# Stick-breaking attention in a long one-core kernel: mask added to the logits, inclusive sums, twelve blocks in three banks, numbered steps, output product by chunks

## What is computed

```python
z = jnp.einsum('bqkgd,bskd->bkgqs', qb, kf)          # qb is scaled by 1/8
mask = key_pos[None, :] < q_pos[:, None]
log_1m_beta = jnp.where(mask, jax.nn.log_sigmoid(-z), 0.0)
rev = lax.cumsum(log_1m_beta, axis=4, reverse=True)
excl = jnp.concatenate([rev[..., 1:], jnp.zeros_like(rev[..., :1])], axis=-1)
a = jnp.where(mask, jnp.exp(jax.nn.log_sigmoid(z) + excl), 0.0)
o = jnp.einsum('bkgqs,bskd->bqkgd', a, vf)
...
x = x + stick_breaking_attention(q, k_shared, v_shared) @ b_w_o[j]
```

## Time and profile before

| | us |
|---|---|
| median of 3 runs | 2183.26 |
| lowest and highest | 2180.99, 2183.5 |
| the profiled execution, its own time | 2183.36 |
| span of its profile (first to last instruction) | 2181.6 |
| mean granted clock of TensorE in it | 0.969 |

### The profile page before, as it was taken

One profiled execution on the slowest core, in us unless ns is written; L12 is line 12 of the kernel. 1 busy time (PEld: TensorE's weight loads), 2 busy tenths in 40 slices (PEclk: granted clock), 3 DMA queues, 4 the chain that ended last, 5 costly groups with the idle time before them and its releaser, 6 DMA issues.

```text
span 2181.6 us, 30498 instructions
## 1 busy us (share of the span) xinstructions
PE 1985.6 (91%) x12952; PEld 1616.1 (74%) x12952; DVE 1114.8 (51%) x1418; ACT 857.3 (39%) x1129; POOL 124.6 (6%) x110
## 2 busy tenths in 40 slices
PE   8999899999999666767689999999999999969998
PEld 8899788889995111111159997889998999958997
DVE  6656584577663101110145555755556555675554
ACT  5534345544343000000034445545445444745443
POOL 0233121000210000000000000000000000030000
PEclk9999999999999989888899999999999999989999
DMA  9533444476987999999985655545554655305552
GB/s 375 169 117 124 149 155 147 163 251 223 314 319 308 423 423 423 423 423 424 421 313 188 235 181 167 174 164 172 186 183 153 203 179 191 116 31 173 192 177 75
DMA packets 242015, 503.17 MB, mean 231 GB/s; under 512 B 9681, under 2 KB 158514, under 8 KB 217426
## 3 DMA queue, kind: packets, MB, share of 16 engines
q1 hardware_dynamic: 241200, 500.27, 63.4%
q10 hardware_dynamic: 530, 0.73, 0.1%
q0 software_dynamic: 144, 0.17, 0.1%
HBM read 500.07 MB, written 1.06 MB: 230 GB/s over the span
## 4 chain that ended last, share of the span: by engine, by line
PE 73%; DMA 16%; DVE 6%; ACT 3%; issue 1%; SPq 0%; POOL 0%; DVEq 0%; ACTq 0%
PE bank L579 21%; PE bank L581 20%; PE bank L580 20%; DMA m<-in_expert_w_up 8%; DMA m<-in_expert_w_gate 7%; PE bank L987 4%; PE bank L732 1%; DVE m L2034 1%; DMA m<-in_ffn_w_in 1%; DVE m L2159 1%; PE bank L874 1%; DVE m L2691 0%; DMA m<-in_ada_w 0%; PE bank L636 0%; ACT m L1408 0%
## 5 line engine op out<-in xcount | busy, mean ns | idle before, releaser
L579 PE MATMUL bank<-m,m 128*128 128x256 f32 (+2 forms) x3240 | 1025.1, 316 | 19.9 <-DVE m L2034 6.9
L580 PE MATMUL bank<-m,m 128*128 128x256 f32 (+2 forms) x3240 | 1010.0, 312 | 0.0
L581 PE MATMUL bank<-m,m 128*128 128x256 f32 (+2 forms) x3240 | 1009.8, 312 | 0.0
L2034 DVE TENSOR_TENSOR m<-m,m 128x1024 fp32r<-128x1024 f32 x508 | 623.1, 1235 | 383.3 <-ACT m L1408 382.7
L1408 ACT ACTIVATE m<-m 128x1024 fp32r<-128x1024 f32 x508 | 531.2, 1056 | 372.5 <-PE bank L581 345.9
L579 PEld LDWEIGHTS bank<-m,m 128*128 128x128 f32 x3240 | 614.9, 190 | 66.2 <-issue 15.4
L580 PEld LDWEIGHTS bank<-m,m 128*128 128x128 f32 x3240 | 615.0, 190 | 37.5 <-issue 2.4
L581 PEld LDWEIGHTS bank<-m,m 128*128 128x128 f32 x3240 | 614.5, 190 | 36.9
L987 PE MATMUL bank<-m,m 128*32 128x512 f32 x1024 | 191.0, 703 | 72.1 <-DMA m<-in_expert_w_up 48.7
L987 PEld LDWEIGHTS bank<-m,m 128*32 128x32 f32 x1024 | 43.4, 124 | 209.6 <-DMA m<-in_expert_w_up 86.7
L998 PE MATMUL bank<-m,m 128*32 128x512 f32 x512 | 91.3, 700 | 32.4 <-DMA m<-in_expert_w_down 26.1
(11 more groups left out here) (353 smaller groups left out, 1367.5 us busy)
## 6 DMA issues: line engine op xcount, KB each, us to landing
m<-in_ffn_w_in SPq DMA_DIRECT2D x88, 1024.0 KB, 5.1
m<-in_expert_w_gate SPq DMA_DIRECT2D x64, 1024.0 KB, 23.9
m<-in_expert_w_up SPq DMA_DIRECT2D x64, 1024.0 KB, 23.8
m<-in_w_in SPq DMA_DIRECT2D x63, 1024.0 KB, 5.1
m<-in_expert_w_down SPq DMA_DIRECT2D x60, 1024.0 KB, 25.0
m<-in_ffn_w_out SPq DMA_DIRECT2D x44, 1024.0 KB, 4.8
m<-in_ada_w SPq DMA_DIRECT2D x24, 1024.0 KB, 5.4
m<-in_a_w_in SPq DMA_DIRECT2D x16, 1024.0 KB, 5.1
```

What stands on the lines that cost most here:

```text
L579: e.matmul(o, s[0], m[0], start=first, stop=False, skip_group_check=skip)
L580: e.matmul(o, s[0], m[1], start=False, stop=False, skip_group_check=skip)
L581: return e.matmul(o, s[1], m[0], start=False, stop=last, skip_group_check=skip)
L2034: inc(e.tensor_tensor(rv(fit(q.L, q.view.shape)), q.view, fit(q.H, q.view.shape), ALU.subtract), "l", skey(q, "L"))
```

## The change

Order of loads: `vv` moves from ahead of `q0` to between `q2` and `q3`; `bo` is loaded and used by halves of its rows, so that its first two pieces need only batch 0, the next two only batch 1, and so on. Steps: each engine has one generator `stick()` with a written list of steps, spawned before `q0`, instead of four batches that start when a query product has ended. Mask: -1e30 is added to the masked logits where they are read from PSUM, so that no mask is applied later. Sums: the matrix is lower triangular with the diagonal (`SLI`), so that z minus the sum is the exponent and the subtraction of the softplus goes. Blocks: the twelve blocks of a batch lie in three full banks of 512 columns. Exp takes |z| with a scale of -1. POOL takes no part any more. The values are summed in one bank. The transposes for `ffn(3)` come after `bo`.

```diff
         for i in range(4):
+            if i == 3:
+                plan_gemm1("vv", wkv, 8, 256, 256, width=256)
             plan_gemm2(f"q{i}", a["b_w_q_2"][0], 8, [256 * i])
-        plan_gemm1("bo", a["b_w_o_2"][0], 8, 0, 1024)
+        for half in range(2):
+            two = [load(... b_w_o_2[0][512 * half:512 * half + 512, 512 * g:512 * g + 512] ...) for g in range(2)]
+            for q in range(2):
+                for g in range(2):
+                    G["bo"].append(Piece(..., g=g, k=4 * half + 2 * q, m=2, end=half == 1 and q == 1))
...
 PE
+                PLACE = (0, 2, 1, 3)
+                def logits(j):
+                    b = [take(4 + i, "sz", j, i) for i in range(3)]
+                    def block(h, u):
+                        r = slice(64 * (h % 2), 64 * (h % 2) + 64)
+                        n = 3 * PLACE[h] + u
+                        return e.matmul(b[n // 4][:, 128 * (n % 4):128 * (n % 4) + 128], k_, qq[r, c:c + 128], ...)
+                    block(2, 1)
+                    then_inc(block(2, 2), "stick", ("szm", j))
+                    for two in (((0, 0), (3, 0)), ((0, 1), (3, 1)), ((0, 2), (3, 2)), ((2, 0), (1, 2))):
+                        for h, u in two:
+                            block(h, u)
+                    w.wait_ge("szm", j)
+                    block(1, 0)
+                    ins = block(1, 1)
+                def sums(j, first):
+                    for n in range(12):
+                        w.wait_ge("ssp", j, n // 6)
+                        ins = e.matmul(o, SLI, sp[:, 128 * n:128 * n + 128], start=True, stop=n % 3 != 1, ...)
+                        if n % 3 == 1:
+                            ins = e.matmul(o, K(C_ONE), sp[:, 128 * n + 128:128 * n + 256], start=False, stop=True, ...)
+                for step in range(15):
+                    if step == 0:
+                        row(nm[1])
+                    if step in (5, 7, 9, 12):
+                        sums(j, 4 if j > 1 else 0)
+                    if step in (8, 10, 12, 14):
+                        values(step // 2 - 4)
+                    if step in (2, 4, 6, 10):
+                        logits((2, 4, 6, 10).index(step))
+                    yield
...
+            ticks.spawn(stick())
             for i in range(4):
-                gemm2(f"q{i}", nm[1].T, m1_ready)
-                if i == 0:
-                    ticks.spawn(batches(sb_batch, ticks))
-            ticks.all = True
+                if i == 3:
+                    values_in()
+                gemm2(f"q{i}", nm[1].T, m1_ready, at=(3, 7, 3, 3)[i])
+            attention_out()
             ticks.join()
-            gemm1("bo", osT, lambda k: ("osT", k // 2), {(1, 4): (nf[3], 0)})
+            enter(nf[3], 0)
             ffn(3)
...
 ACT
+                def shares(j):
+                    inc(e.activation(l_, z_, ACT.Abs), "sb", ("sbt", j))
+                    inc(e.activation(l_, l_, ACT.Exp, scale=-1.0), "sb", ("sbe", j))
+                def logarithm(j):
+                    inc(e.activation(l_, l_, ACT.Ln, bias=1.0), "sb", ("sbl", j))
+                def weights(j):
+                    inc(e.activation(l_, z_, ACT.Exp), "sb", ("sa", j))
+                for step in range(16):
+                    if step in (9, 11, 13, 15):
+                        out_high((step - 9) // 2)
+                    if step in (6, 8, 10, 13):
+                        weights((6, 8, 10, 13).index(step))
+                    if step in (3, 5, 7, 11):
+                        shares((3, 5, 7, 11).index(step))
+                    if step in (4, 6, 8, 11):
+                        logarithm((4, 6, 8, 11).index(step))
+                    yield
...
 DVE
+                def masked(j):
+                    for i in range(3):
+                        taken(e.tensor_tensor(z_[:, 512 * i:512 * i + 512], b[:, :], gone[:, 128 * i:128 * i + 512], ALU.add), ...)
+                def softplus(j):
+                    for q in range(2):
+                        o = slice(768 * q, 768 * q + 768)
+                        inc(e.scalar_tensor_tensor(out=t_[:, o], in0=z_[:, o], scalar=0.0, in1=l_[:, o], op0=ALU.max, op1=ALU.add), ...)
+                def less(j):
+                    for i in range(3):
+                        taken(e.tensor_tensor(z_[:, o], z_[:, o], b[:, :], ALU.subtract), "sc", j, i, ...)
+                for step in range(16):
+                    if step == 0:
+                        row(nm[1])
+                    if step in (5, 7, 9, 12):
+                        softplus((5, 7, 9, 12).index(step))
+                    if step in (6, 8, 10, 13):
+                        less((6, 8, 10, 13).index(step))
+                    if step in (9, 11, 13, 15):
+                        out_low((step - 9) // 2)
+                    if step in (3, 5, 7, 11):
+                        masked((3, 5, 7, 11).index(step))
+                    yield
...
-            e.tensor_copy(mk3[:, 0:128], K(C_SU))
-            e.tensor_copy(mk3[:, 128:256], K(C_ONE))
-            inc(e.tensor_copy(mk3[:, 256:384], K(C_SU)), "sb", ("mk",))
+            for i, c in enumerate((C_SU, C_ONE, C_SU) * 2):
+                e.tensor_scalar(gone[:, 128 * i:128 * i + 128], K(c), -1.0, BIG, ALU.add, ALU.mult)
+            inc(e.tensor_tensor(SLI, K(C_SL), K(C_ID), ALU.add), "sb", ("mk",))
```

More of the change, by code:

```diff
@@ L74, in __init__ @@
     def __init__(self):
-        self.gens, self.ended, self.all = [], set(), False
+        self.gens = []
     def spawn(self, gen, rate=1):
@@ L466, in build @@
               Norm("f2", gain_of(80), xt, halves("xe", 1), row=21504),
-              Norm("f3", gain_of(88), xt, halves("xb"), oT=39456, row=21504)]
+              Norm("f3", gain_of(88), xt, halves("xb"), row=21504)]
         nm = [Norm("m0", gain_of(96), xt, halves("xe", 0)),
@@ L520, in heads @@
                         gens.remove(g)
[L521 to L533, removed]
                 yield
@@ L1222, in mix, with stick @@
                     yield
[L1224 to L1231, removed]
+            def stick():
+                PLACE = (0, 2, 1, 3)
+                def logits(j):
                     w.wait_ge("qq", j)
                     w.wait_ge("kk2", 3)
[L1234 to L1259, removed]
@@ L1260, in sb_batch, with values @@
+                def values(j):
+                    b = take(7, "sbo", j)
+                    w.wait_ge("sa", j)
                     w.wait_ge("vv", 1)
                     v = [vv[:, 256 * i + 64 * j:256 * i + 64 * j + 64] for i in range(2)]
[L1262 to L1265, removed]
+                    for h in range(4):
+                        o, c = slice(64 * (h % 2), 64 * (h % 2) + 64), 256 * (h // 2)
+                        l_ = sbuf[j][0][:, 384 * PLACE[h]:384 * PLACE[h] + 384]
+                        e.matmul(b[o, c:c + 256], v[0], l_[:, 0:256], start=True, stop=False, skip_group_check=True)
+                        ins = e.matmul(b[o, c + 128:c + 256], v[1], l_[:, 256:384], start=False, stop=True,
+                                       skip_group_check=True)
+                    full(ins, "sbo", j)
@@ new lines, in stick, with values_in @@
+                for step in range(15):
+                    if step == 0:
+                        row(nm[1])
+                    if step in (5, 7, 9, 12):
+                        j = (5, 7, 9, 12).index(step)
+                        sums(j, 4 if j > 1 else 0)
[4 more added lines that the diff above has]
+                    yield
+            def values_in():
+                b = take(7, "vv", 0)
+                for p in walk("vv"):
+                    w.wait_ge(*skey(p, "L"))
+                    for i in range(4):
+                        k = p.k + i
+                        w.wait_ge("kv", k // 2)
+                        for t in range(2):
+                            rows = slice(128 * t, 128 * t + 128)
+                            ins = three(b[:, 256 * t:256 * t + 256], (kvT[0][:, k, rows], kvT[1][:, k, rows]),
+                                        parts(p, 256 * i, 256), k == 0 and t == 0, k == 7, True)
+                    used(ins, p, *([("vv", 0)] if p.end else []))
@@ new lines, in attention_out @@
+            def attention_out():
+                o = {}
+                for p in walk("bo"):
+                    w.wait_ge(*skey(p, "L"))
+                    for i in range(2):
+                        k = p.k + i
+                        w.wait_ge("osT", k // 2)
+                        for t in range(2):
+                            if k == 0:
+                                o[p.g, t] = take((3, 0, 1, 2)[2 * p.g + t], "bo", p.g, t)
+                            rows = slice(128 * t, 128 * t + 128)
+                            ins = three(o[p.g, t][:, :], (osT[0][:, k, rows], osT[1][:, k, rows]), parts(p, 512 * i, 512),
+                                        k == 0, k == 7)
+                    used(ins, p, *([("bo", p.g, t) for t in range(2)] if p.end else []))
+                turn["m"] = 3
```

(8 more changed lines are left out.)

185 lines of the change are left out of this document (71 added, 114 removed).

## The result

| | before | after |
|---|---|---|
| median | 2182.43 us (2180.54 to 2187.79, 19 runs) | 2186.73 us (2183.63 to 2189.37, 19 runs) |
| ratio, with its 95% interval | | 1.0019 [1.0011, 1.0026] |
| span of the profiled execution | 2181.6 us | 2183.4 us |
| the stage, `kk`'s end to the first product of `ffn(3)` | 113.2 us | 116.1 us |

The change makes the kernel 0.19% slower: 4.1 us by the ratio, or 2.4 to 5.7 by the interval. The forecast was 1.6 us slower. In the two profiled executions the stage is 2.9 us longer. Behind it both take 199.2 us to the end, and ahead of it the kernel after is 1.1 us shorter (1868.12 against 1869.20), so the 1.2 us that the stage leaves of the 4.1 shows nowhere in these traces; it is smaller than the interval is wide.

What follows compares the result with a forecast made beforehand. A PE-DVE-ACT chain for each batch was taken as the bound, half clock as second cost. The stage summed to 109.8 us plus 5.0 for the clock, 114.8 against 113.2, giving 2184.9 us; 8-in-10 range 2178.5 to 2190.0.

Steps and rivals of the forecast that it cites:

- The bound: Stage from `kk` to `ffn(3)`: a chain from PE to DVE to ACT and back for each batch sets its length.
- To the first sums: From the end of `kk` to the start of sums 0: 28.3 us at full clock, PE waiting 6.8.
- the stall at `kk`: Ahead of the stage, DVE's longer mask building delays transposes and `kk`'s third piece: 0 to 1 us, taken as 0.5.
- A loop: From one batch's sums to the next: 18.7 us, then 19.4 with the evaluation of `q3`; PE's own work 11.2.
- Through `bo`: Sums 2 at 66.4 us, sums 3 at 86.9, then PE works without waits to the end of `bo` at 107.2.
- The end: Behind `bo`, bare transposes for `ffn(3)`: the feed-forward starts 2.1 us later, at 109.3.
- The clock: Half clock behind PE's waits: nothing lost behind the first two, 3.4 to 6.8 us behind the last two, taken as 5.0.
- The sum: Whole stage: 109.8 us at full clock plus 5.0 for half clock, 114.8 against 113.2, or 1.6 us slower.
- The table rule: ACT in the stage: the skill's one set for Exp and Ln gives 105.8 us, the rows' nine loads 114.8.
- The clock spares the chain: Rival for the stage: half clock falls on waits and logits overlap, 108.7 us, 4.5 less, 2178.9; chance 0.20.
- The half clock lasts: Rival for the loops: PE stays at 1.2 GHz and bounds them, stage 122.2 us, 9.0 more, 2192.3; chance 0.17.
- The steps meet: Rival for the stage: every input ready when PE reaches it, PE's work alone, 80.8 us, 32 less; chance 0.02.

Runs made afterwards that it cites:

- e3_fill: Kernel after plus 21 unread 512-column products on PE, filling its waits ahead of the four sums: 2181.61 us, 0.9997 of the kernel before.
- e4_no_loads: Kernel after with Ln replaced by a copy of the same size, leaving one table load of nine: 2177.53 us, 0.9979 of the kernel before.
- e1_steps: Kernel after with the same instructions but step numbers moved on PE, ACT and DVE: 2154.41 us, 0.9872 of the kernel before.
- e10_sub_back: Kernel after with the removed subtraction put back behind the softplus on DVE, result unused: 2190.63 us, 1.0036 of the kernel before.
- e7_clamp: Kernel after with logits held to at most 40 at the mask add, without Abs and DVE's softplus: 2161.65 us, 0.9907 of the kernel before.
- e11_masks: Kernel after with only DVE's mask adds of batches 0 and 1 at earlier steps: 2176.57 us, 0.9978 of the kernel before.

## Why the prediction was right

**The bound** (right). The chain over the three engines sets the stage, not the sum of any: DVE lost 25 us of work and POOL all of its own, and the stage did not shrink.

**To the first sums** (right). 28.8 us with the stall at `kk`; measured 1868.12 to 1897.01, 28.9. The stall was put at 0.5 and is 0.45.

**A loop** (right). 18.7 and 19.4 us; measured 18.46 and 18.96. The second wait came out at 4.42 us, where 7.5 was forecast and 5 to 8 named as the sign: most of the gap is the half clock. Sums 0 took 1897.01 to 1903.06, 6.0 for 3.5, and those 2.5 us came out of the wait and were not added to the loop. The order of operations in the two timelines above is the one written down in the forecast. Logits were taken at 2.0 us and take 1.86 (1877.73 to 1879.59): the pairs overlap nearly as before.

**Through `bo`** (right, sizes a little short). Sums 2 to sums 3 at full clock 20.5; measured 23.46, of which sums 2 at half clock are 2.6 (6.1 for 3.5), so 20.9. From sums 3 to the end of `bo` 20.3; measured 1957.89 to 1981.62, 23.7, less 3.0 for the half clock (sums 3 take 6.5 for 3.5), so 20.7.

**The end** (right, 0.5 short). 2.1 us; measured 1981.62 to 1984.23, 2.6.

**The clock** (right). 5.0 us; 5.6 by the two sections above, 5.3 by e3_fill. The third and fourth waits cost, the first two do not. One reading of the kernel before was wrong: between its first two stretches at half clock it is not all at full clock. A third wait stands there, of 3.98 us, and a stretch at half clock behind it:

```profile
1917.28 0.70 PE L1247 MATMUL bank<-m,m 128*128 128x256 f32 x2 [3.98 <-DVE m L2695]
```

```profile
1918.00:1921.00 3.00, 3.00 (x12) 2.56 (x13) 1.61 (x4) 1.21 (x1) 1.72 (x2) 0.50 0.03 5
```

Nothing in the sum hung on it, as the stage before was taken as measured.

**The sum.** The terms came out +0.1, -0.2, -0.4, +0.4, +0.4, +0.5 and +0.6, each rounded: the stage was forecast at 114.8 and is 116.1. Errors of -0.6 and +2.0 partly cancel, and to that extent the sum is closer by luck. Between the kernel's 4.1 us and the forecast's 1.6 lie this 1.3 and the 1.2 for which the traces show no place. The forecast's 1.6 lies below the interval of 2.4 to 5.7: the size of so small a difference was not forecast, only that two large effects nearly cancel.

**The table rule** (the rows were right). There are nine loads in the stage, groups of ACT after:

```profile
L1819 ACT ACTIVATE m<-m 128x1536 f32<-128x1536 f32 x4 | 5.9, 1484 | 19.0 <-DVE m L2723 19.0
...
L1826 ACT ACT_TABLE_LOAD x4 | 5.1, 1283 | 0.1
L1821 ACT ACT_TABLE_LOAD x3 | 3.8, 1283 | 0.1
L1831 ACT ACT_TABLE_LOAD x2 | 2.6, 1283 | 0.0
```

None stands under L1819, so Abs needs none, as the Trainium skill says (ScalarE: Activation LUTs, Table sets); every Ln has one, which its rule on one set for both functions would spare. What that would be worth is about 9 us, by e4_no_loads (9.1 for eight loads less, Ln itself left out).

**The rivals.** "The clock spares the chain" fell: PE was at half clock behind all four waits. "The half clock lasts" fell: by the rows above a stretch at half clock ends at most 6 us behind its wait (1963.50 against 1957.89), PE is back at full clock by 1903.00, and it waits again ahead of sums 1. "The steps meet" was given 32 us less than before, a stage of 80.8, and a chance of 0.02. The change as made does not do it, but e1_steps comes near, with 84.2 us, 31.5 less than the kernel after and some 28.6 less than before (84.6 with the stall behind `kk`, against 113.2). The argument against it in the forecast was wrong: it took the chain of a batch (over 13 us by ACT's and the splits' rows) as what must fit into one loop of PE's work of 11.2 us. Only one engine's share has to fit. ACT's own work per batch, 8.5 us and two high parts of 1.06, is under 11.2, and once the mask add does not wait for the softplus ahead of it, two batches go through the chain at once.

**Why the change did not pay,** then: removing the subtraction is worth 4.0 us and the early `bo` 7.0, both measured by putting them back into the changed kernel. They are spent on a chain in which every tick puts a high part and a remainder between two operations that wait for each other, and in which two batches never overlap. How the rest of it divides between the Abs, the ticks and the parts of the change that no run undid (the mask in front, the twelve blocks, POOL's leaving) was not measured apart.

## What to carry to other kernels

Where engines work through lists in a fixed order, first write one period of the chain down in order of time over all engines. An operation whose input has long been there but which stands behind one that waits (here the mask add behind the softplus) can be worth more than an operation taken out: three lists renumbered gave 31.5 us of a stage of 115.7 (the half clock that went with the waits included, 5.3 by e3_fill), two operations a batch taken out gave 24.9, and 25 us less of DVE's work than before did not shorten the stage.

Move the lists together: DVE's masks alone gave 9.7 us, PE's list alone 5.7, all three 31.5.

And when the bound has become PE's own work at full clock, stop: two more shortenings brought nothing.

## What the runs showed of the hardware

**A DVE operation beside POOL.** The subtraction put back in e10_sub_back took 1.76 us, while the one of the same shape in the kernel before took 2.55. Timeline of DVE and POOL in the kernel before:

```profile
1902.40 1.84 DVE L2690 TENSOR_TENSOR m<-m,m 128x384 f32<-128x384 f32 x2
1902.44 2.65 POOL L3037 TENSOR_TENSOR m<-m,m 128x384 f32<-128x384 f32 x2 [1274.29 <-DVE m L2687]
...
1904.16 2.55 DVE L2691 TENSOR_TENSOR m<-m,m 128x1536 f32<-128x1536 f32 x1
```

and DVE in e10_sub_back, where POOL does nothing:

```profile
1899.25 1.76 DVE L2735 TENSOR_TENSOR m<-m,m 128x1536 f32<-128x1536 f32 x1
```

POOL's second operation ends at 1905.09, 0.93 us into the subtraction; the subtraction is 0.79 longer than without it. The Trainium skill (SBUF — State Buffer, SBUF: two separate sides) says that a DVE operation with two inputs in SBUF and a POOL operation that reads SBUF lock each other out for a whole instruction. These rows agree with it, though no run here took POOL away from the kernel before. It would also explain why the 2.55 expected of the subtraction in e10_sub_back was too much: there it is 1.76, and the two loops grew by 1.9 each.

**The clock.** In the kernel after, the clock fell to 1.2 GHz near the end of each wait of 4.4 to 6.6 us: ahead of its end for the first, third and fourth (their rows start 1.5, 1.4 and 0.9 us before PE does), just behind it for the second (1.00 up to 1915.50, 0.50 from 1916.00). It stayed there for at least 3 to 5.6 us of PE's work, by the rows of the first fence. In e1_steps, with no wait above 1.6 us in the stage, it was 1.00 throughout. The length of a single wait does not tell by itself: behind one of 2.92 us in e7_clamp the clock was at half (0.50 from 1907 to 1910), behind one of 2.93 in e11_masks it was not (1.00 from 1890 to 1905). The stretch behind the first wait of the kernel after, which cost nothing, is about as long as those behind the third and fourth; what a stretch costs depends on whether PE is in the chain there.
